# The last mixer's projection issued in pieces between its attention steps, and two modulation sums issued between stages

## The chip, the cores and the metric

The kernel runs on one core of a Trainium2 chip. The metric is the device time of one execution in microseconds (us), as the median of several executions; lower is better. In the profile PE is TensorE (matmul; PEld its weight loads), DVE VectorE, ACT ScalarE, POOL GpSimd and SP SyncE, which only issues DMAs here.

## The reference

256 tokens of width 1024 pass through two blocks in f32. The first has two layers, each of a feed-forward, a mixer (HGRN2 in the first layer, forgetting attention, "Fox", in the second) and another feed-forward. The second block is one layer whose norms are modulated by a vector `c`: feed-forward, token mixer, feed-forward. Each of its three sublayers gets shift, scale and gate from `silu(c) @ w_ada + b_ada`:

```python
u = rms_norm(h, norm_pre[i]) * (1 + scale) + shift
h = h + resid_w * gate * rms_norm(fn(u), norm_post[i])
```

The token mixer projects `u` to 5120 columns (`qa, ka, va` of 512, `qd, kd, vd` of 512, `ga, gd` of 1024) and runs two attentions:

```python
ya = stick_breaking_attention(qa, ka, va)      # 8 heads of 64
yd = rms_norm(softmax(q1 k1) v - lam * softmax(q2 k2) v) * (1 - lambda_init)   # 4 heads, value width 128
merged = sigmoid(ga) * (ya @ w_branch_sb) + sigmoid(gd) * (yd @ w_branch_da)
return merged @ w_out
```

The stick-breaking weights need for every score a softplus and a suffix sum over the keys, then an exponential. The differential attention is the difference of two softmaxes with a bias by distance.

## The kernel before, in words

Everything is written out by hand: each engine has one queue of instructions in program order, and semaphores join them. The list of stages (`plan`, L106) is feed-forward, `hg_in`, `hg_out`, feed-forward, feed-forward, `fox_in`, `fox_out`, feed-forward, feed-forward, `tm_in`, `branch`, `tm_out`, feed-forward. The change concerns the end of two feed-forwards (those before `fox_in` and `tm_in`), the head of `fox_in`, and `tm_in` with `branch`.

**A product in three matmuls.** A weight tile of f32 is split: ScalarE rounds `raw` to `w_hi` (L1231, 128x2048), VectorE computes `w_lo = raw - w_hi` (L1714), or GpSimd does so for a few tiles (L479). Activations are split in the same way (`actT_hi`, `actT_lo`). `three` (L542) then issues `hi*w_hi`, `hi*w_lo` and `lo*w_hi` (L544 to L546), 512 columns each. There are four slots of 128x2048 for `raw`, `w_hi` and `w_lo`. SP refills a slot of `raw` once its `w_lo` is made (`free`); ScalarE rounds into `w_hi` again once TensorE is done with the slot (`split_used`).

**A chunk** is 512 output columns of a projection: 2 token tiles x 8 k x 3 = 48 matmuls, with two slots. Even chunks use slots 0 and 1, odd ones 2 and 3. `proj` (L731) runs chunks one after another; the results are copied from PSUM to `tm_p` in SBUF by ScalarE (token tile 0, L1375) and VectorE (tile 1, L1881).

**The Fox mixer** (L900) already has its projection in pieces: `unit(c, t)` is one token tile of one chunk, 24 matmuls, and attention steps stand between units.

**The last mixer.** `tm_in` runs eight chunks in a row in `proj`. Only then does `token_mixer` (L1046) transpose queries and keys (L1057) and start the stick-breaking attention: scores (L1071), softplus on ScalarE (L1575 to L1577) and VectorE (L2189, L2190), suffix sum on TensorE (L1085), mask on VectorE (L2196), exponentials on ScalarE (L1583, L1584), weighing by the values (L1096). Chunks 8 and 9 (the gate `gd`) are issued in eight half-size parts between these steps, in PSUM banks 6 and 7:

```python
gates(3)
for j in range(4):
    if j == 2:
        gates(1)
    sb_suffix(j)
    gates(1)
    sb_weigh(j)
    if j + 2 < 4:
        sb_scores(j + 2)
```

Then come the four heads of the differential attention: scores (L1130, L1132), biased maxima (L2215 to L2220), exponentials (L1612), the difference of the two (L2226 to L2233), transposition (L1144), copy (L1621) and weighing (L1152). There is no other product among them. One branch product follows, the norm of `yd` and its transposition, then the other three branch products (24 matmuls each) and the gating of all results on VectorE (L2268 to L2271), behind one wait for each half. `tm_out` begins with the transposition of the gated result. GpSimd makes `w_lo` for the gate chunk's slots 2 and 3, the four branch slots and the first two slots of `tm_out`.

**The modulation** (`w_ada`) is summed by GpSimd in three pieces, in the background. `ada_reduce(piece)` (L774) turns a piece's sums into columns with 24 matmuls of one column (L782), and VectorE's `modulation` (L1760) adds bias and norm weight. Pieces 0, 1 and 2 are reduced behind the second chunk of the stages with `norm` 3 (a feed-forward), 4 (`fox_in`) and 6 (a feed-forward). `gate_wide_row` (L786) spreads a gate over all partitions. Between two stages TensorE transposes the first normed token tile (`turn_next`, L552), and waits until ScalarE (L1251 or L1245) and VectorE (L1739, L1742 or L1729) have made the two halves of `actT`.

## Time and profile before

| | us |
|---|---|
| median of 3 executions | 1776.73 |
| lowest, highest | 1772.1, 1778.73 |
| the profiled execution | 1771.41 |
| its span, first to last instruction | 1769.7 |
| TensorE busy (matmul) | 1677.7 |
| VectorE busy | 1012.8 |
| ScalarE busy | 825.3 |
| GpSimd busy | 607.4 |
| mean granted clock of TensorE | 0.974 |

All rows come from the profiled execution. Its time is 1.7 us over its span, and 5.3 us under the median. The clock is given as a share of 2.4 GHz; it has two levels, 1.0 and 0.5 (1.2 GHz). A matmul's own duration (0.39 us) overlaps with the next one's, so costs are read from the distance of starts. The last mixer's first product starts at 1333.7, its second chunk ends at 1365, its eighth at 1430.1; `tm_out` starts at 1538.7 and its last product ends at 1568.1.

### The profile page before, as it was taken

How to read it: one execution, taken by the hardware profiler on the slowest of the kernel's cores; microseconds unless marked ns; L12 is line 12 of the kernel's file. 1: busy time of each engine (PE TensorE's matmuls, PEld its weight loads, DVE VectorE, ACT ScalarE, POOL GpSimd, SP SyncE). 2: the span in 40 equal slices, each digit the busy share in tenths (PEclk: the TensorE clock that was granted, in tenths of full speed). 3: DMA queues.
4: the chain of work that ended last, by engine and by line, in shares of the span. 5: the costliest groups of instructions: out<-in, count | busy, mean ns of one | idle time of the engine just before them, and what ended most of it. 6: DMA issues, size and time to landing. Idle time of an engine off the chain costs nothing.

```text
span 1769.7 us, 21737 instructions
## 1 busy us (share of the span) xinstructions
PE 1677.7 (95%) x7909; PEld 1387.4 (78%) x7909; DVE 1012.8 (57%) x993; ACT 825.3 (47%) x970; POOL 607.4 (34%) x376
## 2 busy tenths in 40 slices
PE   6999999999999999989999999999998986889998
PEld 5888788878887888877887888788876864778886
DVE  4554568676556555666657565645456425465454
ACT  5555552353445344445455443534444355454443
POOL 0000000088888888860018898500000021500000
PEclk9999999999999999989999999999998997899999
DMA  6656453267776677852437778365554521326552
GB/s 215 214 189 197 159 190 107 84 210 253 246 258 218 219 236 243 272 170 96 144 100 236 240 242 273 128 199 189 182 197 134 196 99 46 120 95 213 190 182 79
DMA packets 208279, 321.44 MB, mean 182 GB/s; under 512 B 10920, under 2 KB 146402, under 8 KB 208226
## 3 DMA queue, kind: packets, MB, share of 16 engines
q1 hardware_dynamic: 195968, 281.05, 48.4%
q0 software_dynamic: 10512, 38.54, 7.0%
q10 hardware_dynamic: 1746, 1.11, 0.2%
q8 instruction: 36, 0.59, 0.1%
q14 instruction: 17, 0.14, 0.0%
HBM read 319.62 MB, written 1.05 MB: 181 GB/s over the span
## 4 chain that ended last, share of the span: by engine, by line
PE 85%; DVE 8%; ACT 4%; issue 2%; DMA 0%; ACTq 0%; SPq 0%; DVEq 0%
PE ps L544 25%; PE ps L546 24%; PE ps L545 24%; DVE w_lo L1714 3%; PE ps L648 2%; PE ps L844 1%; ACT w_hi L1231 1%; PE ps L590 1%; PE ps L782 1%; DVE x L1780 1%; PE ps L597 1%; ACT arena L1262 1%; PE ps L976 1%; DVE actT_lo L1729 1%; DVE arena L1748 1%
## 5 line engine op out<-in xcount | busy, mean ns | idle before, releaser
L1714 DVE TENSOR_TENSOR w_lo<-raw,w_hi 128x2048 fp32r<-128x2048 f32 x258 | 653.0, 2540 | 328.6 <-ACT w_hi L1231 328.0
L544 PE MATMUL ps<-w_hi,actT_hi 128*128 128x512 f32 x1504 | 603.0, 401 | 22.0 <-DVE actT_lo L1742 7.8
L1231 ACT CAST w_hi<-raw 128x2048 fp32r<-128x2048 f32 x266 | 505.6, 1911 | 193.4 <-PE ps L546 190.8
L546 PE MATMUL ps<-w_hi,actT_lo 128*128 128x512 f32 x1504 | 592.1, 394 | 0.0
L545 PE MATMUL ps<-w_lo,actT_hi 128*128 128x512 f32 x1504 | 591.2, 393 | 0.0
L544 PEld LDWEIGHTS ps<-w_hi,actT_hi 128*128 128x128 f32 x1504 | 286.5, 191 | 82.6 <-DVE actT_lo L1729 9.0
L546 PEld LDWEIGHTS ps<-w_hi,actT_lo 128*128 128x128 f32 x1504 | 285.6, 190 | 61.9
L545 PEld LDWEIGHTS ps<-w_lo,actT_hi 128*128 128x128 f32 x1504 | 286.8, 191 | 57.0
L544 PE MATMUL ps<-w_hi,hT_hi 128*128 128x512 f32 x480 | 187.5, 391 | 2.6 <-DVE hT_lo L1839 2.6
L546 PE MATMUL ps<-w_hi,hT_lo 128*128 128x512 f32 x480 | 186.8, 389 | 0.0
L545 PE MATMUL ps<-w_lo,hT_hi 128*128 128x512 f32 x480 | 186.8, 389 | 0.0
L497 POOL DMA_DIRECT2D arena<-w_ada_dram x72 | 66.7, 926 | 325.8 <-PE ps L552 279.6
L508 POOL TENSOR_TENSOR arena<-arena 128x512 f32<-128x512 f32 x72 | 161.8, 2247 | 5.6
L505 POOL TENSOR_TENSOR arena<-arena,c_silu 128x1024 f32<-128x1024 f32 x72 | 152.8, 2123 | 11.8 <-DMA arena<-w_ada_dram 9.4
L479 POOL TENSOR_TENSOR w_lo<-raw,w_hi 128x2048 fp32r<-128x2048 f32 x8 | 36.7, 4601 | 341.7 <-ACT w_hi L1231 341.6
L1328 ACT CAST hT_hi<-ps 128x512 fp32r<-128x512 f32 x60 | 35.2, 587 | 233.9 <-PE ps L648 233.9
L510 POOL TENSOR_TENSOR arena<-arena 128x256 f32<-128x256 f32 x72 | 119.5, 1660 | 5.6
L544 PEld LDWEIGHTS ps<-w_hi,hT_hi 128*128 128x128 f32 x480 | 90.1, 188 | 21.6 <-DVE hT_lo L1839 3.0
L546 PEld LDWEIGHTS ps<-w_hi,hT_lo 128*128 128x128 f32 x480 | 90.1, 188 | 18.9
L545 PEld LDWEIGHTS ps<-w_lo,hT_hi 128*128 128x128 f32 x480 | 90.1, 188 | 18.5
L1839 DVE TENSOR_TENSOR hT_lo<-ps,hT_hi 128x512 fp32r<-128x512 f32 x60 | 41.4, 691 | 94.8 <-ACT hT_hi L1328 94.8
L1334 ACT ACTIVATE gate<-ps 128x256 f32<-128x256 f32 x66 | 25.3, 384 | 148.9 <-PE ps L546 130.2
(254 smaller groups left out, 1397.4 us busy)
## 6 DMA issues: line engine op xcount, KB each, us to landing
raw<-ffn_w_in_dram SPq DMA_DIRECT2D x176, 512.0 KB, 4.8
raw<-ffn_w_out_dram SPq DMA_DIRECT2D x88, 512.0 KB, 4.4
arena<-w_ada_dram POOLq DMA_DIRECT2D x72, 512.0 KB, 5.4
raw<-ffn_w_gate_dram SPq DMA_DIRECT2D x44, 512.0 KB, 4.0
raw<-ffn_w_up_dram SPq DMA_DIRECT2D x44, 512.0 KB, 4.9
raw<-ffn_w_down_dram SPq DMA_DIRECT2D x44, 512.0 KB, 4.3
raw<-w_in_dram SPq DMA_DIRECT2D x40, 512.0 KB, 4.5
raw<-hg_w_in_dram SPq DMA_DIRECT2D x32, 512.0 KB, 4.7
```

Of the source, the lines that this page charges most:

```text
L479: nc.gpsimd.tensor_tensor(w_lo[:, s, :], raw[:, s, :], w_hi[:, s, :].bitcast(F32), ALU.subtract)\
L497: nc.gpsimd.dma_start(ada_raw[:, s, :, :], w_ada[:, :, bass.ds(piece * ADA_W + u * ADA_U, ADA_U)])\
L505: nc.gpsimd.tensor_tensor(r, r, c_silu[:, :].unsqueeze(2).to_broadcast([P, KD, ADA_U]), ALU.mult)\
L508: nc.gpsimd.tensor_tensor(r[:, 0:4, :], r[:, 0:4, :], r[:, 4:8, :], ALU.add).then_inc(ada_by4, 1)
L510: nc.gpsimd.tensor_tensor(r[:, 0:2, :], r[:, 0:2, :], r[:, 2:4, :], ALU.add).then_inc(ada_by2, 1)
L544: nc.tensor.matmul(to, hi, whi, start=start, stop=False, skip_group_check=True)
L545: nc.tensor.matmul(to, hi, wlo, start=False, stop=False, skip_group_check=True)
L546: return nc.tensor.matmul(to, lo, whi, start=False, stop=stop, skip_group_check=True)
L648: last = nc.tensor.transpose(ps[:, HT_BANK, f * T + t * P:f * T + (t + 1) * P], hidden[:, t, f * P:(f + 1) * P], ident)
L1231: nc.scalar.copy(w_hi[:, s, :], raw[:, s, :]).then_inc(hi_ready[s], 1)
L1714: nc.vector.tensor_tensor(w_lo[:, s, :], raw[:, s, :], w_hi[:, s, :].bitcast(F32), ALU.subtract)\
L1839: nc.vector.tensor_tensor(hT_lo[:, :, :], ps[:, HT_BANK, :].rearrange("p (f t) -> p f t", f=2), hT_hi[:, :, :].bitcast(F32), ALU.subtract) ...
```

## The change

`tm_in`, `branch` and the attention become one hand-written order on each engine.

- TensorE issues chunks 2 to 9 as 16 units of 24 matmuls in banks 6 and 7, with attention steps between them, and the branch as eight units of 12 matmuls. The first transposition for `tm_out` stands inside the last of these.
- All `w_lo` of the stage are made by VectorE; GpSimd makes none.
- The results of chunks 8 and 9 are copied like all others and the sigmoids are taken in SBUF, for each half of the gates apart. Gating on VectorE goes by branch unit.
- The stick-breaking result is first copied to SBUF (`ya_raw`), and rounded into `actT_hi` only after the last unit of its token tile, since `actT_hi` is read by the projection till then.
- The buffers of scores and weights move in `arena`, and the branch's weights are loaded in another order of slots (both halves of `w_branch_sb` first).
- `ada_reduce(0)` and `ada_reduce(2)` go from behind the second chunk of two feed-forwards to the end of the feed-forwards before `fox_in` and `tm_in`, after `turn_next`. VectorE's `modulation(0)`, `(1)` and `(2)` go to the mixers' queues.

```diff
@@ SP: the branch's slots
-                        n = slice(COLS * (s // 2), COLS * (s // 2) + COLS)
+                        n = slice(COLS * (s % 2), COLS * (s % 2) + COLS)
...
-                            nc.sync.dma_start(to[:, ks, :], branch_w[s % 2][:, ks, n]).then_inc(raw_loaded[s], 16)
+                            nc.sync.dma_start(to[:, ks, :], branch_w[s // 2][:, ks, n]).then_inc(raw_loaded[s], 16)
@@ GpSimd
-            split_gate_weights(by_name["tm_in"])
-            for s in (0, 2, 1, 3):
-                split_lo(s, by_name["branch"].filled[s])
-            for s in (0, 1):
-                split_lo(s, by_name["tm_out"].filled[s])
@@ TensorE: the sums
             def after_second_chunk(st):
                 if st.norm >= 6:
                     pe.wait_ge(gate_row_ready, st.norm - 6 + 1)
-                if st.norm in (3, 4, 6):
-                    ada_reduce({3: 0, 4: 1, 6: 2}[st.norm])
+                if st.name == "fox_in":
+                    ada_reduce(1)
...
                 turn_next(st, 0)
+                nxt = following[id(st)]
+                if nxt is not None and nxt.kind == "in" and nxt.norm > 1:
+                    ada_reduce(0 if nxt.name == "fox_in" else 2)
@@ TensorE: token_mixer
+                def unit(c, t):
...
+                    i, b = c // 2, c % 2
+                    if c > 2:
+                        pe.wait_ge((kept0, kept1)[t], st.kept + c)
+                    for s in (2 * b, 2 * b + 1):
+                        pe.wait_ge(lo_ready[s], st.filled[s] + i + 1)
+                        for kk in range(4):
+                            k, w = 4 * (s % 2) + kk, slice(kk * COLS, (kk + 1) * COLS)
+                            last = three(ps[:, 6 + t, :], actT_hi[:, k, tok], actT_lo[:, k, tok],
+                                         w_hi[:, s, w], w_lo[:, s, w], k == 0, k == KD - 1)
...
+                first_chunk(st, [acc(0, t) for t in range(TILES)], proj0_done)
+                after_first_chunk(st)
+                pe.wait_ge(lam_one, 1)
+                nc.tensor.matmul(ps[:, 5, 0:1], C["ones"][0:1, :], lam_one_col, start=True, stop=True).then_inc(lam_wide, 1)
+                chunk(st, 0, 1)
+                after_second_chunk(st)
```

The new order on TensorE, one call of the code after another (`wait_kept` and the waits inside the calls left out):

```text
unit(2,0) turn(0,4) turn(512,2) unit(2,1) sb_scores(0) sb_scores(1) unit(3,0) sb_suffix(0) unit(3,1) sb_suffix(1)
sb_weigh(0) unit(4,0) sb_scores(2) sb_weigh(1) unit(4,1) sb_scores(3) unit(5,0) sb_suffix(2) unit(5,1) sb_suffix(3)
sb_weigh(2) unit(6,0) sb_weigh(3) turn(1536,0) turn(2048,2) unit(6,1) da_scores(0) da_scores(1) unit(7,0) da_turn(0)
unit(7,1) da_weigh(0) da_turn(1) da_scores(2) unit(8,0) da_weigh(1) da_scores(3) unit(8,1) da_turn(2) unit(9,0)
da_weigh(2) da_turn(3) unit(9,1) da_weigh(3) branch_unit(0,0,0) (0,1,0) (0,0,1) (0,1,1) turn_yd()
branch_unit(1,0,0) (1,1,0) (1,0,1) (1,1,1) with turn_tile(tm_out, 0) inside
```

On ScalarE (`weights(c)` rounds the two slots of chunk c, `keep(c)` copies its tile 0):

```text
weights(1) keep(0) wide weights(2) keep(1) queries(1) weights(3) keep(2) softplus(0) softplus(1) weights(4) keep(3)
sb_weights(0) weights(5) sb_weights(1) keep(4) softplus(2) weights(6) softplus(3) keep(5) sb_weights(2) weights(7)
sb_weights(3) keep(6) keep_ya() queries(3) weights(8) da_weights(0) da_weights(1) keep(7) turned_probs(0) weights(9)
turned_probs(1) da_weights(2) keep(8) da_weights(3) gates(0) split_hi branch 0, 1 turned_probs(2) keep(9) round_ya(0)
turned_probs(3) load_sqrt round_ya(1) squares split_hi branch 2 std split_hi branch 3 gates(1) split_hi out 0 yd_hi
split_hi out 1 turn(out, 0) turn(out, 1) split_hi out 2, 3 turn(out, 2) turn(out, 3)
```

On VectorE (`weights(c)` makes the two `w_lo` of chunk c, `keep(c)` copies its tile 1, which needs the end of `unit(c,1)`; `gated(n, half, t)` gates a branch unit):

```text
modulation(2) weights(1) keep(0) lambda weights(2) keep(1) keys(2) weights(3) keep(2) softplus(0) softplus(1)
weights(4) mask(0) keep(3) mask(1) weights(5) softplus(2) keep(4) softplus(3) weights(6) mask(2) keep(5) mask(3)
weights(7) keys(4) keep(6) weights(8) biased_max(0) biased_max(1) difference(0) keep(7) difference(1) weights(9)
biased_max(2) keep(8) biased_max(3) difference(2) split_lo branch 0 rest_ya(0) difference(3) split_lo branch 1
keep(9) rest_ya(1) mean gated(0,0,0) normed yd gated(0,1,0) split_lo branch 2 gated(0,0,1) split_lo branch 3
gated(0,1,1) yd_lo split_lo out 0 gated(1,0,0) gated(1,1,0) split_lo out 1 turn(out, 0) turn(out, 1) gated(1,0,1)
gated(1,1,1) split_lo out 2, 3 turn(out, 2) turn(out, 3)
```

In the Fox mixer VectorE's queue now begins with `modulation(0)`, and `modulation(1)` stands where the one call was.

## Rows read from the trace of the kernel before

**Rows 1.** the page, part 4: the chain that ended last, by engine

```profile
PE 85%; DVE 8%; ACT 4%; issue 2%; DMA 0%; ACTq 0%; SPq 0%; DVEq 0%
```

**Rows 2.** windows: us; PE, PEld, DVE, ACT, POOL busy (instructions); clock; DMA share; GB/s

```profile
771.00:925.00 154.00, 150.74 (x785) 126.91 (x786) 93.22 (x98) 77.24 (x125) 20.24 (x12) 0.94 0.38 125
1365.00:1430.10 65.10, 65.10 (x289) 53.75 (x287) 30.55 (x18) 24.05 (x17) 0.00 (x0) 1.00 0.59 203
1430.10:1538.70 108.60, 80.14 (x423) 63.84 (x422) 46.10 (x78) 64.61 (x94) 36.73 (x8) 0.88 0.23 78
1487.00:1510.00 23.00, 14.14 (x56) 10.53 (x57) 11.06 (x28) 11.83 (x28) 9.03 (x2) 0.50 0.13 47
1538.70:1568.10 29.40, 26.99 (x113) 21.70 (x114) 15.95 (x18) 14.76 (x22) 0.00 (x0) 0.90 0.12 36
```

**Rows 3.** waits of PE in 1333 to 1540: total us, times, longest

```profile
PE ps L1144 <- DVE arena L2233: 6.7, 2, 4.2
```

**Rows 4.** ACT in the last mixer: a group, and its timeline (start, us)

```profile
L1231 ACT CAST w_hi<-raw 128x2048 fp32r<-128x2048 f32 x9 | 16.9, 1898 | 2.9 <-PE ps L546 2.9
...
1437.53 0.81 ACT L1575 ACTIVATE arena<-ps 128x768 f32<-128x768 f32 x1 [2.27 <-PE ps L1073]
...
1442.56 0.79 ACT L1575 ACTIVATE arena<-ps 128x768 f32<-128x768 f32 x1
...
1518.50 3.73 ACT L1642 ACTIVATE arena<-arena 128x2048 f32<-128x2048 f32 x2
```

**Rows 5.** timeline of DVE in the last mixer

```profile
1365.68 4.49 DVE L1714 TENSOR_TENSOR w_lo<-raw,w_hi 128x2048 fp32r<-128x2048 f32 x2
...
1430.48 0.69 DVE L1881 COPY arena<-ps 128x512 f32 x1 [5.79 <-PE ps L546]
...
1481.05 0.95 DVE L2215 TENSOR_TENSOR arena<-ps,arena 128x768 f32<-128x768 f32 x1
...
1483.15 0.95 DVE L2215 TENSOR_TENSOR arena<-ps,arena 128x768 f32<-128x768 f32 x1
...
1486.32 0.75 DVE L2233 SCALAR_TENSOR_TENSOR arena<-arena,small 128x128 f32<-128x128 f32 x2
```

**Rows 6.** the chain in the last mixer, a suffix sum (start, us)

```profile
1455.28 1.97 PE ps L1085 x12
```

**Rows 7.** timeline of PE, differential scores of two heads

```profile
1479.43 0.50 PE L1130 MATMUL ps<-arena 64*128 64x128 f32 x4
...
1480.19 0.49 PE L1130 MATMUL ps<-arena 64*128 64x128 f32 x4
```

**Rows 8.** window of PE's clock in the Fox mixer

```profile
899.00:906.00 7.00, 7.00 (x27) 6.13 (x27) 2.66 (x5) 0.00 (x0) 0.00 (x0) 0.52 0.65 208
```

**Rows 9.** groups of the last mixer with GpSimd at work

```profile
L479 POOL TENSOR_TENSOR w_lo<-raw,w_hi 128x2048 fp32r<-128x2048 f32 x8 | 36.7, 4601 | 341.7 <-ACT w_hi L1231 341.6
...
L2271 DVE TENSOR_TENSOR arena<-arena 128x512 f32<-128x512 f32 x4 | 6.2, 1543 | 0.1
```

**Rows 10.** the page, part 6: weight loads, us to landing

```profile
raw<-w_in_dram SPq DMA_DIRECT2D x40, 512.0 KB, 4.5
```

**Rows 11.** the chain at the three modulation sums

```profile
580.03 5.25 PE ps L782 x48
...
787.63 7.72 PE ps L782 x48
...
1147.80 6.22 PE ps L782 x48
```

**Rows 12.** windows behind a sum and at the gaps between stages

```profile
585.00:589.00 4.00, 4.00 (x15) 3.38 (x15) 3.60 (x4) 2.38 (x2) 3.63 (x3) 0.57 0.37 107
757.00:762.00 5.00, 0.58 (x5) 0.34 (x3) 4.71 (x7) 2.35 (x7) 4.06 (x4) 0.73 0.26 61
1327.00:1334.00 7.00, 1.11 (x9) 0.87 (x8) 6.86 (x12) 3.81 (x10) 0.00 (x0) 0.67 0.47 150
1334.00:1340.00 6.00, 6.00 (x16) 4.66 (x16) 2.56 (x6) 0.53 (x2) 0.00 (x0) 0.53 0.01 3
```

More of the change, by code:

```diff
@@ L1157, in token_mixer @@
+                unit(6, 0)
+                sb_weigh(3)
+                wait_kept(5)
+                turn(1536, 0)
+                turn(2048, 2)
+                unit(6, 1)
                 da_scores(0)
                 da_scores(1)
[L1159 to L1166 removed]
@@ L1187, in branch @@
-            def branch(st):
-                branch_part(st, 0, 1)
-                pe.wait_ge(yd_ready, 2)
-                for half in range(HALF):
-                    branch_part(st, 1, half)
+                unit(7, 0)
+                da_turn(0)
+                unit(7, 1)
+                da_weigh(0)
+                da_turn(1)
+                da_scores(2)
+                unit(8, 0)
+                da_weigh(1)
+                da_scores(3)
+                unit(8, 1)
+                da_turn(2)
@@ new lines, in token_mixer @@
+                unit(9, 0)
+                da_weigh(2)
+                da_turn(3)
+                unit(9, 1)
+                da_weigh(3)
+                for t in range(TILES):
+                    for half in range(HALF):
+                        branch_unit(0, half, t)
+                turn_yd()
+                branch_unit(1, 0, 0)
+                branch_unit(1, 1, 0)
+                branch_unit(1, 0, 1)
+                branch_unit(1, 1, 1, lambda: turn_tile(by_name["tm_out"], tm_p[:, :, 3072:4096], 0))
@@ new lines, in gates @@
+                def gates(n):
+                    for t in range(TILES):
+                        act.wait_ge((kept0, kept1)[t], st.kept + 8 + 2 * n)
+                        g = tm_p[:, t, 3072 + n * D:3072 + (n + 1) * D]
+                        nc.scalar.activation(g, g, ACT.Sigmoid).then_inc(tm_gates, 1)
+                weights(1)
+                keep(0)
+                wide(st)
+                weights(2)
+                keep(1)
+                queries(1, 4, tm_qaT)
+                weights(3)
@@ new lines, in token_mixer @@
+                keep(2)
+                softplus(0)
+                softplus(1)
+                weights(4)
+                keep(3)
+                sb_weights(0)
+                weights(5)
+                sb_weights(1)
+                keep(4)
+                softplus(2)
+                weights(6)
+                softplus(3)
+                keep(5)
+                sb_weights(2)
+                weights(7)
+                sb_weights(3)
+                keep(6)
+                keep_ya()
@@ L1644, in vectors @@
+                turn(nxt, 3)
             def vectors():
@@ new lines, in token_mixer @@
+                modulation(2)
+                weights(1)
+                keep(0)
+                dve.wait_ge(lam_wide, 1)
+                nc.vector.tensor_scalar(neg_lam_col, ps[:, 5, 0:1], -1.0, None, ALU.mult).then_inc(lam_ready, 1)
+                weights(2)
+                keep(1)
+                keys(2, 2, tm_kaT)
+                weights(3)
+                keep(2)
+                softplus(0)
+                softplus(1)
+                weights(4)
+                mask(0)
+                keep(3)
@@ L2236, in token_mixer @@
+                mask(1)
+                weights(5)
+                softplus(2)
+                keep(4)
+                softplus(3)
+                weights(6)
+                mask(2)
+                keep(5)
+                mask(3)
+                weights(7)
+                keys(4, 2, tm_kdT)
+                keep(6)
+                weights(8)
                 dve.wait_ge(bias_loaded, 16)
-                dve.wait_ge(sb_y, 4)
                 dve.wait_ge(lam_ready, 1)
```

507 lines of the change are left out of this document (245 added, 262 removed).

## The prediction, made before the changed kernel was run

> **What bounds the kernel now.** I read the chain that ended last first, to see which engine sets the end: it is TensorE for 85% of the span [rows 1]. So a microsecond counts only if TensorE waits less, runs less at the lower of its two clocks, or has less to do. Then I read windows of the last mixer. In the last six chunks of its projection TensorE is never idle: 288 matmuls of 512 columns in 65.1 us [rows 2] are 0.226 us each, 5.4 us for a "unit" of 24 (one token tile of one chunk of 512 columns). Behind them come 108.6 us in which TensorE is busy for 80.1, so idle for 28.5, at a mean clock of 0.88 [rows 2]. Most of the low clock (0.5, which is 1.2 GHz) lies in 1487 to 1510: 14.1 us of work at 0.50 [rows 2], of which half, 7 us, is lost, and some 1 us more at the edges. Together **36.5 us are lost** in a stage with about 72 us of work. The waits say why: the attention's exponentials, maxima and masks on ScalarE and VectorE are a serial chain, and TensorE has only two gate chunks and the first branch product to put between its links. The longest are at the transposes of the probabilities, L1144: 6.7 us behind VectorE's difference [rows 3], and one of 6 us beside it.
>
> **Part 1, the projection in pieces.** Nothing is added to TensorE: the same 480 projection and 96 branch matmuls, the same small steps. What changes is that the gaps can be filled with 16 units instead of 8 half-size pieces. The gain is 36.5 us less what the new order still loses. I walk the three written queues with durations of this trace.
>
> Durations: ScalarE rounds a weight slot in 1.9 us, and a softplus step (magnitude, exponential, logarithm, two table loads) takes 5.0 (1437.53 to 1442.56) [rows 4]. VectorE subtracts a slot in 2.25 us and copies a tile of 512 columns in 0.7; a biased maximum takes 2.1 us (1481.05 to 1483.15), a maximum and a difference together 3.9 (to 1487.07), so 1.8 for the difference [rows 5]. The suffix sum takes TensorE 2.0 us [rows 6], the differential scores of a head 0.76 [rows 7].
>
> Stick-breaking part. TensorE puts unit 3,0, suffix 0, unit 3,1 and suffix 1 (14.9 us) between the scores of the second pair of heads and the first weighing. The other side needs two softplus steps (10, begun 0.8 earlier), chunk 4's weights (3.8 on ScalarE, the last 2.25 on VectorE behind it), then a mask (0.7) and exponentials (0.9): 17. TensorE waits 2.1 there and 0.6 before suffix 0. From there to unit 6,0 I find every step early.
>
> Differential part. Here the order is tight, because VectorE now also has all the low halves.
> - After unit 6,1, VectorE has a copy (0.7), two slots (4.5), two maxima (4.2) and a difference (1.8): 11.2. TensorE has two scores (1.5) and unit 7,0 (5.4). It waits 4.3 at the first transposition.
> - After unit 7,1: copy and difference (2.5) against a weighing (about 0.7): 1.8.
> - After unit 8,1: copy, maximum, difference (4.6) against nothing, since the transposition of head 2 comes next: 4.6.
> - After unit 9,0: ScalarE's queue holds the last exponentials (about 2), the first sigmoids (1.3 load, and 1.9, half of the 3.7 of [rows 4]), two slots (3.8) and a copy ahead of what TensorE wants: 1.6. Then copy, rounding of the first attention's result, its low half and a difference, over two engines: 3.1.
> - Before the second branch product, ScalarE's second sigmoids and one slot stand ahead of the rounding of the turned result: 1.5.
>
> These are **19.6 us of waiting**, against 36.5 lost before: 16.9 gained. TensorE's clock then falls where it has too little to do. A fall in the Fox mixer lasted all of 899 to 906 [rows 8], 7 us, 3.5 lost. For my waits I take 5 us, between 0 (no fall) and 10 (three falls). Net 11.9.
>
> GpSimd's eight low halves (4.6 us each [rows 9]) go to VectorE as eight more of 2.25, 18 us; VectorE was busy for 46 of 108.6 and 31 of 65.1 us [rows 2], so it is full only in the places above. While GpSimd ran, a 128x512 addition on VectorE averaged 1.5 us [rows 9], where a copy of the same size takes 0.7; the walk takes every duration from stretches without GpSimd. The Trainium skill, SBUF — State Buffer, "Who interferes with whom", has the two engines lock one port pair; rows 9 agree, and it speaks for the change.
>
> Weight transfers move with the low halves that free their slots; by the walk a slot is free 10 us or more before its next rounding, against 4.5 us for landing [rows 10], so I cost them at nothing. SP's queue keeps its order of slots. If one came late, its unit would wait for all of the lateness.
>
> The first output product starts hot, with its source already turned inside the last branch unit. Of its 29.4 us, at a clock of 0.90 [rows 2], I take off 4: 0.90 is 6 us at the low level, 3 lost, and some 1 of waiting for weights and residual. The lambda matmul and the maxima's bias load only change place.
>
> **Part 2, two modulation sums moved.** The 24 one-column matmuls took 5.25 us at 580 and 6.22 at 1147.8 on the chain [rows 11]. The clock fell behind the first (585 to 589 at 0.57 [rows 12]: 3.4 us low, 1.7 lost); I take the same for the second. Removed: 14.9. Their new place is the gap between feed-forward and mixer, where TensorE waits for the turned activations (it is busy for 0.58 of 757 to 762 and 1.11 of 1327 to 1334 [rows 12]). The means of 0.73 and 0.67 there put the fall of the clock at 759.3 and 1329.4. At 787.63 the same 24 took 7.7 us [rows 11], with the fall inside them at about 790.5; that makes 0.22 each before it (as at 580) and 0.43 behind. Started at 757.2 and 1327.6, 10 and 8 run before the fall and the rest behind it: they end about 3.5 and 2.6 us after the moment (761.8, 1333.7) at which the product starts now. Bounds: nothing at all, and 5.9 and 4.4 (all at the low rate, 10.3). I take 6.1, so part 2 gives 8.8. VectorE's three small operations per sum go to the head of its mixer queue; they take well under 1 us, and chunk 1's low halves are ready over 1 us early, so nothing, and 1 us if not.
> The Trainium skill, TensorE: Matmul & The Clock Gate, "What's actually happening", says that the throttle is the default state and activity releases it. Taken so, the sums would hold the clock up through the gap. Rows 11 and 12 don't agree: it fell during or right behind such sums. It is a rival below.
>
> **Sum.** 11.9 + 4 + 8.8 = 24.7 off the profiled execution's 1771.4 gives 1746.7. That execution lies 5.3 under the median of the three runs, 1776.7, so the median should be **1752**.
>
> **Rivals.**
> - *TensorE stays fed.* The Fox mixer has the same form, and in 154 us TensorE is idle for only 3.3 there at a clock of 0.94 [rows 2] (18 us low, 9 lost): 12 lost. If this mixer did as well, the 24.6 that I leave it become 12: gain 37, 1739. Against it: my waits are sums of rows on one queue.
> - *The sums keep the clock up.* They end 0.6 us late at most, and the 4 to 5 us at the low level behind each gap (1334 to 1340 at 0.53 [rows 12]) go too, half of it gained: 5.5 and 4.6, some 10 more, 1742. Against it are the falls at 585 and 790.
> - *Falls of clock everywhere.* Each of eight waits brings a 7 us fall: 28 lost instead of 5, the change is worth 2, 1775.
> - *Slower.* VectorE becomes the bound of every chunk: low halves stand behind softmax steps that themselves wait for TensorE's next step, so slots, of which each has one buffer, are freed late in turn. Place: chunks 2 to 9. Were each to wait for one unit and a rounding (5.4 + 1.9), 58 us would be lost, against 49 that there are to win (36.5, 4, 8.8): 1786. It decides from 6.2 us per chunk. VectorE's busy shares above speak against it.
>
> **Chances.** Forecast (gain 13 to 33) 0.60, fed 0.20, clock held 0.08, falls everywhere 0.07, slower 0.05. The measurement can tell about 0.5%, 9 us. The range goes from the fed case with the sums hidden (37 and 6: 1733) to the upper costs of clock (5 more), gaps (4) and a slip of 8 in the walk: gain 8, 1769. Faster 0.88, same 0.07, slower 0.05.
>
> **What would show it.** In the profile after: waits of about 4, 2, 5 and 3 us at the probabilities' transposes, released by VectorE's difference, and one near 2 at the first weighing; GpSimd idle after its sums; from the end of chunk 1 (1365.0) to the first output product 162 us instead of 173.7; the moved sums in the gaps, with the product 3 us later behind them. Wrong it would be if TensorE hardly waits, if a transfer is what releases units, or if the clock stays low after the first wait.

## The result, and the profile of the changed kernel

The changed kernel takes **1752.3 us** (median of 4 executions, 1750.6 to 1754.6) against 1775.4 for the kernel before in the same session (4 executions): a ratio of 0.9875, 95% interval 0.9855 to 0.9895, so 23 us less (19 to 26). A second session (e11 below) gave 0.9858 (0.9832 to 0.9885). The forecast was 1752. But it was not right term by term, and the runs below show why. The profiled execution takes 1751.1 us with a span of 1749.4. Against the profiled execution before (1771.4) that is 20.3 us less: 6.7 up to the end of chunk 1, 8.7 in the mixer, 4.0 in the output product and 0.9 behind it.

The page's chain of work that ended last, by engine, answers to [rows 1]:

```profile
PE 64%; POOL 20%; DVE 6%; issue 5%; ACT 3%; POOLq 1%; DMA 0%; ACTq 0%; SPq 0%; DVEq 0%
```

It says 20% for GpSimd where it had none. TensorE is as busy as ever (1678.1 us, 96%). What is new is one link in the Fox mixer, at which TensorE waits for GpSimd. Behind it the chain follows GpSimd's own work back for hundreds of microseconds. The share is large, but its price is only the wait, 0.42 us in this execution (below).

Windows of the changed kernel; the columns are those of [rows 2]. The first runs from the end of chunk 1 to the first output product, which were 173.7 us in the kernel before. The second is the output product, 29.4 before. The last two are the stretches of the two gaps:

```profile
1358.30:1523.30 165.00, 147.70 (x709) 119.04 (x708) 88.32 (x101) 91.25 (x115) 0.00 (x0) 0.93 0.37 126
...
1523.30:1548.70 25.40, 23.91 (x114) 19.68 (x113) 17.88 (x22) 15.06 (x22) 0.00 (x0) 1.00 0.23 74
...
750.00:770.00 20.00, 19.45 (x97) 16.92 (x95) 8.09 (x19) 5.94 (x20) 17.02 (x15) 0.74 0.45 140
1318.00:1345.00 27.00, 24.82 (x112) 21.23 (x113) 19.05 (x34) 11.86 (x25) 0.60 (x1) 0.75 0.20 69
```

In the mixer TensorE is idle for 17.3 us (165.0 less 147.7), where it was for 28.5. Yet it is busy for longer than the 145.2 us of before (65.10 and 80.14 in [rows 2]), with the same work: the clock costs more than it did. The stretches at the low level between 1358.3 and 1523.3 of the changed kernel are these, with the one such stretch of the mixer before behind them (windows of two kernels):

```profile
1390.60:1394.00 3.40, 3.40 (x13) 2.50 (x10) 2.19 (x1) 3.40 (x3) 0.00 (x0) 0.50 0.88 330
1445.20:1452.00 6.80, 5.11 (x14) 4.15 (x15) 1.53 (x6) 2.77 (x10) 0.00 (x0) 0.50 0.12 47
1458.80:1462.30 3.50, 3.50 (x11) 2.36 (x8) 3.50 (x3) 0.06 (x1) 0.00 (x0) 0.51 0.32 90
1475.90:1482.70 6.80, 4.47 (x12) 3.68 (x13) 2.13 (x8) 6.17 (x12) 0.00 (x0) 0.50 0.00 0
1489.60:1493.00 3.40, 3.03 (x9) 2.55 (x10) 2.52 (x2) 1.97 (x3) 0.00 (x0) 0.50 0.12 44
```

```profile
1486.40:1510.30 23.90, 14.45 (x57) 10.75 (x58) 11.96 (x29) 12.43 (x30) 9.03 (x2) 0.50 0.13 45
```

TensorE was busy for 19.5 us at half speed, so 9.7 us were lost; before it was 14.4 us, so 7.2 were lost. The same work at the full clock takes 138.0 us by either kernel (147.7 less 9.7, 145.2 less 7.2). The output product starts hot, at a clock of 1.00, and takes 25.4 us.

Waits of PE from 1315 to 1560 in the changed kernel (us in total, times, longest), which answer to [rows 3]:

```profile
PE ps L1096 <- DVE arena L2245: 13.2, 4, 4.6
...
PE ps L1072 <- ACT arena L1574: 1.9, 1, 1.9
PE ps L532 <- DVE actT_lo L2337: 1.7, 1, 1.7
PE ps L1059 <- DVE arena L2211: 0.5, 1, 0.5
```

L1096 is the transposition of the probabilities, L2245 VectorE's difference. One by one, from the timeline of PE (start, us, the wait and its releaser in brackets):

```profile
1446.89 0.90 PE L1096 MATMUL ps<-consts_sb,arena 128*128 128x128 f32 x3 [3.80 <-DVE arena L2245]
...
1457.79 0.55 PE L1096 MATMUL ps<-consts_sb,arena 128*128 128x128 f32 x3 [1.84 <-DVE arena L2245]
...
1478.23 0.90 PE L1096 MATMUL ps<-consts_sb,arena 128*128 128x128 f32 x3 [4.61 <-DVE arena L2245]
...
1489.97 0.90 PE L1096 MATMUL ps<-consts_sb,arena 128*128 128x128 f32 x3 [2.97 <-DVE arena L2245]
```

The walk had 4.3, 1.8, 4.6 and 3.1. The reader should also see the 0.90 us that three of the four transpositions take, against 0.55 for the other: they run at the low clock.

VectorE in the mixer, now without GpSimd beside it (groups from 1358 to 1523, columns as in [rows 9]). The addition of the gated halves, 128x512 with both sources in SBUF, is back at 0.69 us from 1.54. The multiplications ahead of it, with one source in PSUM (L2263), take the 0.68 that they took beside GpSimd before (L2268 and L2269 there):

```profile
L1741 DVE TENSOR_TENSOR w_lo<-raw,w_hi 128x2048 fp32r<-128x2048 f32 x20 | 45.1, 2287 | 8.0 <-ACT w_hi L1240 7.9
...
L2263 DVE TENSOR_TENSOR arena<-arena,ps 128x512 f32<-128x512 f32 x6 | 4.1, 686 | 2.8 <-PE ps L534 2.8
...
L2267 DVE TENSOR_TENSOR arena<-arena 128x512 f32<-128x512 f32 x2 | 1.4, 692 | 0.1
```

The two sums that stayed visible, piece 1 in the Fox mixer and piece 2 in its new gap, from the chain; they answer to [rows 11]:

```profile
788.98 6.55 PE ps L740 x48
...
1319.37 7.25 PE ps L740 x48
```

### The profile page after: what moved, and what is told of

It reads as the page before. It is cut to its first block, busy times and chain, and to the rows that moved or that the text cites. A ratio compares the mean times of both kernels' runs of the same rounds, so it can differ in the third digit from the quotient of the medians.

```text
span 1749.4 us, 21688 instructions
## 1 busy us (share of the span) xinstructions
PE 1678.1 (96%) x7909; PEld 1387.5 (79%) x7909; DVE 1022.2 (58%) x1003; ACT 826.2 (47%) x973; POOL 570.5 (33%) x368
## 4 chain that ended last, share of the span: by engine, by line
PE 64%; POOL 20%; DVE 6%; issue 5%; ACT 3%; POOLq 1%; DMA 0%; ACTq 0%; SPq 0%; DVEq 0%
PE ps L532 18%; PE ps L534 18%; PE ps L533 18%; POOL arena L501 6%; POOL arena L498 6%; POOL arena L503 4%; POOL arena L505 3%; DVE w_lo L1741 2%; PE ps L802 1%; PE ps L638 1%; POOL arena L490 1%; ACT w_hi L1240 1%; PE ps L578 1%; PE ps L740 1%; PE ps L934 1%
## 5 line engine op out<-in xcount | busy, mean ns | idle before, releaser
L1741 DVE TENSOR_TENSOR w_lo<-raw,w_hi 128x2048 fp32r<-128x2048 f32 x266 | 668.8, 2524 | 333.2 <-ACT w_hi L1240 333.1
L532 PE MATMUL ps<-w_hi,actT_hi 128*128 128x512 f32 x1504 | 605.1, 402 | 10.1 <-DVE actT_lo L1756 3.2
L503 POOL TENSOR_TENSOR arena<-arena 128x256 f32<-128x256 f32 x72 | 115.9, 1609 | 5.6
L1869 DVE TENSOR_TENSOR hidden<-gate,ps 128x256 f32<-128x256 f32 x132 | 54.3, 416 | 54.4 <-ACT gate L1343 48.0
```

Of the source, the lines that this page charges most:

```text
L503: nc.gpsimd.tensor_tensor(r[:, 0:2, :], r[:, 0:2, :], r[:, 2:4, :], ALU.add).then_inc(ada_by2, 1)
L532: nc.tensor.matmul(to, hi, whi, start=start, stop=False, skip_group_check=True)
L1741: nc.vector.tensor_tensor(w_lo[:, s, :], raw[:, s, :], w_hi[:, s, :].bitcast(F32), ALU.subtract)\
L1869: nc.vector.tensor_tensor(hidden[:, t, :], gate[:, t, :], ps[:, UP_BANK + t, FC:COLS], ALU.mult)\
```

## The experiments

Each ratio is to the kernel before, run in the same session; 0.001 is 1.8 us. "Changed" is the changed kernel.

| run | what | median us | ratio, 95% |
|---|---|---|---|
| changed | | 1752.3 | 0.9875 (0.9855 to 0.9895) |
| e11 | changed again | 1753.7 | 0.9858 (0.9832 to 0.9885) |
| e1 | part 2 alone (sums) | 1766.2 | 0.9949 (0.9928 to 0.9971) |
| e2 | part 1 alone (mixer) | 1759.7 | 0.9912 (0.9898 to 0.9926) |
| e3 | transpositions later | 1735.6 | 0.9779 (0.9763 to 0.9794) |
| e4 | e3, difference first | 1732.1 | 0.9738 (0.9720 to 0.9757) |
| e5 | low halves on GpSimd | 1762.9 | 0.9922 (0.9904 to 0.9939) |
| e6 | wide matmuls among the sums | 1756.0 | 0.9897 (0.9879 to 0.9915) |
| e7 | e2, gaps filled wide | 1754.3 | 0.9871 (0.9848 to 0.9894) |
| e8 | modulation behind low halves | 1754.3 | 0.9870 (0.9840 to 0.9901) |
| e9 | e8, piece 1 shortened | 1747.7 | 0.9831 (0.9815 to 0.9847) |
| e10 | e4's orders on e7 | 1733.6 | 0.9757 (0.9739 to 0.9775) |
| e12 | waits filled wide | 1742.7 | 0.9823 (0.9802 to 0.9844) |

e11 is the changed kernel without an edit, in the session of e9, e10 and e12:

> The changed kernel once more, unchanged, as the common measure of the experiments: ratio 0.9875 to the kernel before, within 0.002. If its ratio comes out outside of that, the differences of 2 to 4 us between the experiments (e6, e7, e8 against the changed kernel) are not to be read.

Measured: within 0.002, so the table can be read down to some 3 us, and no finer.

For the mixer there is a second measure, the time from its first transposes to those ahead of the output product. It was 157.46, 157.40 and 157.49 us in the traces of changed, e2 and e11. But it isn't always the same: in e8, whose orders in the mixer and whose four waits at the transpositions (3.80, 1.83, 4.61, 2.98) are those of changed, it was 152.16, because the clock fell two times instead of five:

```profile
1371.39:1523.55 152.16, 134.83 (x671) 109.02 (x670) 86.74 (x98) 89.63 (x112) 0.00 (x0) 0.97 0.39 132
```

So waiting can be read from a trace to a tenth of a microsecond, but what the clock costs differs between executions by up to some 5 us.

**Do the parts add up? e1 and e2.** e1 has only the moved sums, with VectorE's operations on them (not shown here):

```diff
-                if st.norm in (3, 4, 6):
-                    ada_reduce({3: 0, 4: 1, 6: 2}[st.norm])
+                if st.name == "fox_in":
+                    ada_reduce(1)
...
+                if nxt is not None and nxt.kind == "in" and nxt.norm > 1:
+                    ada_reduce(0 if nxt.name == "fox_in" else 2)
```

> The kernel before with part 2 alone: the modulation sums of pieces 0 and 2 stand behind the feed-forward stages, and VectorE's three operations for each stand at the head of its queue in the next mixer; the mixer is as before. If the two parts add up, and the mixer's new order does not need the moved sums, this gives what the trace of the changed kernel shows at the four places: 6.9 us removed and some 4.5 given back in the Fox mixer, 8.4 removed and 1.2 given back at the last mixer, so about 9.6 us off the kernel before (ratio about 0.995); the prediction had 8.8. Rival: the moved sums also bring the low clock forward into the first chunk, and that part of the saving of the changed kernel which lies in the last mixer's first chunk came from the new order; then 5 us or less (ratio 0.997 or more).

e2 is the changed kernel with just that undone.

> The changed kernel with part 2 undone: the sums of pieces 0 and 2 stand again behind the second chunk of the feed-forward stages. If the parts add up, this is slower than the changed kernel by the 9.6 us of part 2, so some 13 us off the kernel before (ratio about 0.9925): 8.6 in the mixer and 4.1 in the output product. The prediction had 15.9 for the two. Rival: the two parts overlap (both take from the same low clock in the first chunk of the last mixer), and this alone gives over 17 us.

Measured: 9.1 us (5 to 13) and 15.6 us (13 to 18). The sum, 24.7, lies between the two measurements of both together (22 and 25), so no overlap of the parts can be seen, within intervals of 3 and 4 us. The part sizes of the prediction were 8.8 and 15.9.

**The waits at the transpositions: e3 and e4.** e3 changes only TensorE's order:

```diff
                 unit(7, 0)
-                da_turn(0)
                 unit(7, 1)
+                da_turn(0)
+                unit(8, 0)
                 da_weigh(0)
                 da_turn(1)
                 da_scores(2)
-                unit(8, 0)
+                unit(8, 1)
                 da_weigh(1)
                 da_scores(3)
-                unit(8, 1)
-                da_turn(2)
                 unit(9, 0)
+                da_turn(2)
+                unit(9, 1)
                 da_weigh(2)
                 da_turn(3)
-                unit(9, 1)
                 da_weigh(3)
```

> The changed kernel, on TensorE alone in another order of the same steps: of each head's transposition of the probabilities and its weighing, every one stands about one projection unit later (unit 7,1 ahead of the transposition of head 0, the scores of head 2 behind unit 8,0, the transposition of head 2 behind unit 9,0 with unit 9,1 behind it). If the waits at the transpositions (13.2 us in four) are VectorE's queue being half a unit to a unit behind, they fall to about 4, and the clock falls once or twice less: 9 to 13 us below the changed kernel (ratio to the kernel before about 0.981). Rival 1: exponentials, difference, transposition and copy are a chain of fixed length that TensorE waits for whole at its end; then the wait moves to the last weighing or the first branch product, and the time stays within 2 us of the changed kernel. Rival 2: most is lost by the clock after any wait, however short; then the waits fall but 24 us at the low clock stay, and the gain is some 5.

Measured: 17 us below changed by the ratio (0.9779 against 0.9875), 14 against e11. That is more than the expectation asked, and both rivals are out. The waits of PE at L1096 went from 13.2 us in four to one:

```profile
PE ps L1096 <- DVE arena L2245: 2.5, 1, 2.5
```

The same stretch with the same 672 matmuls, from the first transposes to those ahead of the output product, in changed and in e3 (windows of two kernels):

```profile
1363.71:1521.17 157.46, 140.16 (x672) 112.70 (x670) 86.75 (x98) 89.76 (x112) 0.00 (x0) 0.92 0.37 127
```

```profile
1368.55:1508.37 139.82, 132.58 (x672) 107.55 (x670) 86.92 (x98) 89.21 (x112) 0.00 (x0) 0.99 0.42 143
```

It is 17.6 us shorter: 10.1 of them are waiting (17.3 less 7.2), and 7.6 are the same matmuls in less busy time at a clock of 0.99 instead of 0.92. Of the 7.6, 1.7 belong to the fall at 1390 in changed, behind the first weighing, where e3 altered nothing: the wait of 1.9 us there was followed by a fall in six of the twelve traces with this mixer (changed, e2, e4, e6, e9, e11) and by none in the others. That leaves some 6 for the moved steps, so a wait here cost about 1.6 times its length. By e8 it can be less: behind the same 13.2 us of waits TensorE lost 4.0 us by the clock there, where it lost 8.0 in changed.

e4 puts VectorE's last difference first as well:

```diff
+                difference(3)
                 split_lo(0, mix.filled[0])
                 rest_ya(0)
-                difference(3)
```

> The kernel with the later transpositions (e3), and on VectorE the difference of head 3 ahead of the low half of the first branch slot and of the first attention's low halves, instead of behind them. In e3 TensorE still waited 2.5 us for that difference and 0.6 for the copy behind it. If that wait is the queue order, it goes (2.5 to 3 us below e3, whose median was 1735.6). Rival: the low halves that now come later are what the first branch unit needs, and it waits there for as long: no change, or 1 us slower.

Measured: 3.5 us below e3 by the medians, 7 by the ratios of two sessions; in the trace the stretch is 137.06 us instead of 139.82, so 2.8. The queue order was the cause of the wait of 2.5, and the first branch unit did not wait. The 0.6 us behind it stayed.

**What the clock costs by itself: e12.** TensorE waits as before, but does useless wide work meanwhile:

```diff
                 def da_turn(h):
+                    pe.wait_ge(da_max, h + 1)
+                    for _ in range((14, 6, 16, 10)[h]):
+                        nc.tensor.matmul(ps[:, 2 * (h % 2), :], hT_hi[:, 0, 0:P],
+                                         hT_hi[:, :, :].rearrange("p f t -> p (f t)"), start=True, stop=True)
                     pe.wait_ge(da_p, 2 * (h + 1))
```

> The changed kernel with 14, 6, 16 and 10 useless 512-column matmuls (3.2, 1.4, 3.6 and 2.3 us at the full clock) in the four waits at the transpositions of the probabilities (3.8, 1.8, 4.6 and 3.0 us), so that TensorE is busy while the same differences are awaited. This separates what a wait costs by itself from what the clock costs behind it: if the four falls between 1446 and 1493 (20 us at the low clock, some of it inside the waits) come from the waits, they go, and the kernel is 4 to 8 us faster than the changed one with as long a wait for VectorE. Rival: the narrow steps around the waits are enough for the falls; then the fillers run at the low clock too, last longer than the waits, and the kernel is up to 3 us slower.

Measured, in the same session as e11: 6 us below it by the ratios, 11 by the medians. The stretch takes 149.79 us, 7.7 less, at a clock of 1.00:

```profile
1357.43:1507.22 149.79, 142.23 (x717) 114.29 (x716) 86.74 (x98) 89.56 (x112) 0.00 (x0) 1.00 0.39 134
```

So none of the 9.7 us that the clock took in changed are lost here: 8.0 of them lay behind the four waits, and 1.7 behind the first weighing, where nothing was filled and this trace has no fall. Some 2 us of the gain went again, since the fillers with the waits that are left take longer than the waits took: TensorE still waits 2.0 us at the transpositions, and 1.5 at a weighing where it didn't in changed. That the 7.7 here and the 7.6 of e3 are so close is chance.

**Queue length or shared port: e5.** GpSimd makes the low halves of chunks 8 and 9:

```diff
+            for s in range(SLOTS):
+                n = by_name["tm_in"].filled[s] + 4
+                pool.wait_ge(hi_ready[s], n + 1)
+                nc.gpsimd.tensor_tensor(w_lo[:, s, :], raw[:, s, :], w_hi[:, s, :].bitcast(F32), ALU.subtract)\
+                    .then_inc(lo_ready[s], 1)
...
-                weights(8)
...
-                weights(9)
```

> The changed kernel with the low halves of the last two projection chunks (8 slots' worth in two chunks: 4 subtractions of 2.25 us on VectorE) made by GpSimd again, 4.6 us each and out of VectorE's queue. If VectorE's queue length makes the waits at the probabilities' transpositions (4.6, 4 and so on: 13.2 in four), the first and the one behind chunk 9's weights each lose up to 4.5 us, so about 5 to 8 us of waiting go and the time falls by as much. Rival: VectorE runs slower while GpSimd runs (a 128x512 operation took 1.5 us instead of some 0.7 in the kernel before), and the copies, maxima and differences of this stretch give back most of it: 0 to 3 us faster, or slower.

Measured: 8 to 11 us slower than changed, as the rival had it ("or slower"). The waits grew to 19.4 us. The first fell from 3.8 to 3.0, the second grew from 1.8 to 8.9, and the other two stayed:

```profile
PE ps L1101 <- DVE arena L2250: 19.4, 4, 8.9
```

The timelines of GpSimd and VectorE in e5, and of VectorE for the same head in changed, tell why (start, us, operation):

```profile
1456.68 8.98 POOL L529 TENSOR_TENSOR w_lo<-raw,w_hi 128x2048 fp32r<-128x2048 f32 x2 [8.59 <-ACT w_hi L1245]
```

```profile
1457.97 0.17 DVE L2243 RECIPROCAL small<-small 128x4 f32<-128x4 f32 x1
1458.17 3.06 DVE L2244 TENSOR_SCALAR small<-small 128x2 f32<-128x2 f32 x1
1461.26 4.74 DVE L2247 TENSOR_SCALAR arena<-arena,small 128x128 f32<-128x128 f32 x2
1466.04 0.75 DVE L2250 SCALAR_TENSOR_TENSOR arena<-arena,small 128x128 f32<-128x128 f32 x2
```

```profile
1455.93 0.17 DVE L2238 RECIPROCAL small<-small 128x4 f32<-128x4 f32 x1
1456.13 0.23 DVE L2239 TENSOR_SCALAR small<-small 128x2 f32<-128x2 f32 x1
1456.40 0.55 DVE L2242 TENSOR_SCALAR arena<-arena,small 128x128 f32<-128x128 f32 x2
1456.99 0.75 DVE L2245 SCALAR_TENSOR_TENSOR arena<-arena,small 128x128 f32<-128x128 f32 x2
```

An operation on 128x2 elements takes 3.06 us instead of 0.23: it ends at 1461.2, where the first of GpSimd's two subtractions ends, and the next stands until the second has ended near 1465.7. VectorE isn't slowed in proportion, it is held until GpSimd's instruction is over. The Trainium skill, SBUF — State Buffer, "Who interferes with whom", says of VectorE's two-port modes that whoever issues first has the shared pair for the whole instruction and the other "fully blocks". This trace agrees as to the blocking; in which mode the operations ran it doesn't show.

**The gaps: e6 and e7.** e6 puts a useless 512-column matmul behind every third sum:

```diff
+                    if fill and u % 3 == 1:
+                        nc.tensor.matmul(ps[:, UP_BANK, :], hT_hi[:, 0, 0:P],
+                                         hT_hi[:, :, :].rearrange("p f t -> p (f t)"), start=True, stop=True)
```

> The changed kernel, with a 512-column matmul of no use (feed-forward values on both sides, into a bank that nothing reads) behind every third of the 24 one-column matmuls of the two moved sums: 8 more per sum, 1.8 us at the full clock. If one-column matmuls and waiting are what lets TensorE's clock fall in these gaps, and wide matmuls hold it, the sum with its filler ends after 7.1 us (now 7.55 and 7.25) and the first chunk behind it runs at the full clock instead of losing some 3 us: 5 to 8 us below the changed kernel in all. Rival: the clock falls as before, by the wait or by the share of narrow work; then each sum takes 1.8 to 3.5 us more, all of it behind the moment at which the activations are there: 3 to 7 us slower than the changed kernel.

Measured: 0.9897, so 4 us slower than changed, or 7 than e11. The intervals overlap, so "slower" isn't shown; but the gain of 5 to 8 us isn't there. The traced execution is the fastest of e6's four (1747.8). Even in it the clock falls inside the mixed stretch of the second gap, which begins at 1316 (windows of e6):

```profile
1316.00:1320.00 4.00, 4.00 (x29) 3.77 (x29) 3.93 (x7) 1.25 (x4) 0.00 (x0) 0.87 0.45 123
1320.00:1329.00 9.00, 9.00 (x34) 8.04 (x34) 4.56 (x12) 2.58 (x7) 0.60 (x1) 0.50 0.26 76
```

e7 has the sums in their old places and 26 such matmuls, one behind the other, in each gap:

```diff
                 turn_next(st, 0)
+                if st.norm in (3, 6):
+                    for _ in range(26):
+                        nc.tensor.matmul(ps[:, UP_BANK, :], hT_hi[:, 0, 0:P],
+                                         hT_hi[:, :, :].rearrange("p f t -> p (f t)"), start=True, stop=True)
```

> The kernel with only the mixer's part of the change (e2), with 26 useless 512-column matmuls, 5.9 us at the full clock, in the two gaps between feed-forward stage and mixer in place of waiting; the sums stand in their old places. If it is the idle time there, or the narrow work of the sums, that lets the clock fall, it now stays up through the gap and the first chunk behind it: 3 to 7 us less in each gap, 1750 to 1753 against 1759.7 for e2. Rival: the fall is already caused by the wait of 1.7 us and the eight transposes at the end of the feed-forward stage, ahead of the filler; then the filler itself runs partly at the low clock, ends after the moment at which the activations are there, and the time is equal to that of e2 or up to 4 us more.

Measured: 1754.3 against 1759.7 for e2 in another session (5 us less; 0.9871 against 0.9912, 7 us less). The clock stays up through both gaps; these windows of e7 answer to the 0.74 and 0.75 shown above. The 0.94 is a fall from 1340 on, behind a later wait of 1.9 us; until then the second one has 1.00:

```profile
750.00:770.00 20.00, 20.00 (x98) 16.58 (x97) 9.85 (x20) 8.27 (x23) 16.89 (x15) 1.00 0.59 184
1318.00:1345.00 27.00, 23.37 (x100) 18.05 (x99) 20.59 (x35) 14.62 (x31) 0.00 (x0) 0.94 0.21 71
```

The wait of 1.7 us and the eight transposes ahead of the filler are the same in e7 as in changed, so they didn't bring the fall by themselves; it came where narrow sums (changed) or idle time (e2) stood behind them. The Trainium skill, TensorE: Matmul & The Clock Gate, "What's actually happening", says that activity releases the throttle. With wide matmuls that agrees; with one-column matmuls, and with three of them to one wide one, TensorE was busy for some nine tenths of the time or more in the rows here, and the clock fell.

**What became of the gain in the Fox mixer: e8 and e9.** e8 changes VectorE's order, for piece 0 and piece 2 alike:

```diff
-                modulation(0)
                 weights(1)
+                modulation(0)
                 keep(0)
```

> The changed kernel with VectorE's three operations on the sums of pieces 0 and 2 behind the low halves of the mixer's second chunk instead of ahead of them. In the changed kernel's Fox mixer TensorE waited 1.6 to 1.9 us for a low half in chunk 1, which the prediction had at nothing. If these operations at the head of the queue (they wait for the end of the sum, and hold the low halves back) are the cause, the wait goes, and the kernel is up to 2 us faster. Rival: the low halves are late because VectorE runs slower beside GpSimd there; then the wait stays as it was.

Measured: the same time as changed. In changed the first product on those low halves waited 1.58 us, and VectorE's three small operations took 3.0 (timelines of PE and VectorE):

```profile
777.37 0.50 PE L532 MATMUL ps<-w_hi,actT_hi 128*128 128x512 f32 x1 [1.58 <-DVE w_lo L1741]
```

```profile
770.94 0.17 DVE L1790 TENSOR_TENSOR modc<-ps,cols 128x24 f32<-128x24 f32 x1
771.14 2.66 DVE L1793 SCALAR_TENSOR_TENSOR mod_scale<-modc,cols 128x8 f32<-128x8 f32 x1
773.83 0.17 DVE L1795 SCALAR_TENSOR_TENSOR mod_gate<-modc,cols 128x8 f32<-128x8 f32 x1
```

The second began while GpSimd issued a transfer (770.90 to 771.83), and stood until the multiplication behind it, which ran from 771.85 to 773.76, had ended. So both stories have part of it: the operations are at the head of the queue, and they are slow beside GpSimd. It depends on the moment. In six of the eight traces with this order the second operation took 2.25 to 2.66 us and TensorE waited 1.1 to 1.6. In e11, which is the same kernel, and in e4 it fell between two of GpSimd's instructions, and TensorE didn't wait (VectorE in e11):

```profile
770.12 0.17 DVE L1790 TENSOR_TENSOR modc<-ps,cols 128x24 f32<-128x24 f32 x1
770.32 0.17 DVE L1793 SCALAR_TENSOR_TENSOR mod_scale<-modc,cols 128x8 f32<-128x8 f32 x1
770.52 0.17 DVE L1795 SCALAR_TENSOR_TENSOR mod_gate<-modc,cols 128x8 f32<-128x8 f32 x1
```

With e8's order that wait is gone too, but the time came back, a small part in the last mixer (0.9 us before the matmuls that spread the gate, L748, for `mod_gate`, which now comes later), most of it at the next wait, the sums of piece 1, which wait for GpSimd. The timeline of PE there in changed, e11 and e8:

```profile
788.98 6.55 PE L740 MATMUL ps<-consts_sb,arena 128*128 128x1 f32 x48 [0.42 <-POOL arena L505]
```

```profile
788.16 10.40 PE L740 MATMUL ps<-consts_sb,arena 128*128 128x1 f32 x48 [2.28 <-POOL arena L505]
```

```profile
792.48 10.40 PE L740 MATMUL ps<-consts_sb,arena 128*128 128x1 f32 x48 [6.74 <-POOL arena L505]
```

Near the end of the Fox mixer nothing is left of what the first moved sum gave: transposes which stand there in both kernels begin at 906.72 in the traces of before and of changed alike.

e9 shortens GpSimd's last two partial sums of piece 1. It leaves out seven eighths of the products in these two, so its modulation isn't that of the reference, and its time is only a bound for what is to be had here:

```diff
-                    ada_unit(piece, ADA_N // 2 - 1, s)
+                    ada_unit(piece, ADA_N // 2 - 1, s, piece == 1)
```

> The kernel with VectorE's modulation operations behind the low halves (e8), and the last two of GpSimd's 24 partial sums of piece 1 computed from a small part of their data (an eighth of the products, and the additions over them shortened alike), so that this part of the last mixer's modulation is left out; GpSimd ends piece 1 some 5 us earlier. In the changed kernel and in e8 TensorE waited 0.4 and 6.7 us for GpSimd at the sums of piece 1 (0.4 to 6.7 in the ten traces), and the clock was low for up to 20 us behind that. If GpSimd is what caps the gain of part 2 in the Fox mixer, that wait goes and the time is 5 to 8 us below e8 (1754.3): 1746 to 1749. Rival: TensorE meets another wait within the next steps (the forget gates' chain on ScalarE and VectorE), or the clock falls by the narrow sums alone: within 2 us of e8.

Measured: 1747.7, 7 us below e8 by the ratios, and in the same session 6 below e11 by the medians, 5 by the ratios. The intervals overlap in either comparison, so the size isn't sure. In its trace PE doesn't wait at these sums, though they still take 7.85 us, partly at the low clock; that is its slowest execution (1754.7), and TensorE waits 2.5 us for `mod_gate` in the last mixer. So GpSimd's piece 1 is what the earlier TensorE runs into; that its removal is worth 5 to 7 us is likely, but not shown. Where the wait is 2.3 us or more, the sums behind it take 10.40 us, all at the low clock, instead of 6.55.

Executions of one kernel with moved sums lie up to 19 us apart (e1: 1758.1 to 1777.4; e11: 1744.6 to 1759.6), those of the kernel before within 9 in a session. The moments at GpSimd may be one cause, the falls of the clock in the mixer (e8) another; e7, without moved sums, has 11 us too. Only one execution of each has a trace, so that stays open.

**The best of both: e10.** e7 with the orders of e3 and e4.

> All together but the moved sums: later transpositions and the earlier difference (e4), and the wide useless matmuls in the two gaps with the sums in their old places (e7). e7 was as fast as the changed kernel, so moving the sums and holding the clock are worth the same; if the parts add up this takes what e4 took, 1731 to 1735. Rival: e7 was at its time only by the clock's luck, and this is 1737 or more.

Measured: 1733.6, as added up. Against e4 the ratios differ by 0.002, less than their intervals. e4 and e10 both beat both kernels, by 2.6% and 2.4% to the kernel before. e4 is the simpler one, and computes nothing useless.

## Why the prediction was right, point by point

- **The total.** 24.7 us forecast, 23 measured by the medians; by parts 15.9 and 8.8 against 15.6 and 9.1, with intervals of some 3 and 4 us. That the median comes out at 1752 itself is partly luck. The sum was made for the profiled execution, 1746.7, and that took 1751.1: 20.3 us less, not 24.7 (mixer 8.7 for 11.9, output product 4.0 for 4, before them 6.7 for 8.8). The 5.3 us which were put on for the median were 1.2 in the changed kernel. Where the medians gained the rest no trace shows.
- **The mixer's waits.** 19.6 us forecast, 17.3 idle. The four at the transpositions were 3.80, 1.84, 4.61, 2.97 for 4.3, 1.8, 4.6, 3.1; the first weighing 1.9 for 2.1, suffix 0 0.5 for 0.6, the second branch product 1.7 for 1.5. Only the 1.6 before the weighing of head 2 didn't come. The cause was right too: e3 and e4 took the waits at the transpositions away by order alone.
- **The clock in the mixer: the term that was mis-sized.** "For my waits I take 5 us, between 0 (no fall) and 10": it took 9.7 in the traces of changed and e11, 8.0 of it behind the four waits. Its upper bound was three falls of 7 us; there were five, of 3.4 or 6.8 us. In e8 it took 4.0 with the same waits, so within its bounds the term is also a matter of the execution. The 8 us taken for the kernel before were 7.2. So 35.7 us were lost before (28.5 and 7.2) and 27.0 after (17.3 and 9.7). Idle time gave 11.2 instead of 8.9, and the clock took 2.5 instead of giving 3: 8.7 instead of 11.9.
- **The output product.** 4 forecast, 29.4 to 25.4 measured, at a clock of 1.00 as said.
- **The sums in the gaps.** Ends 3.5 and 2.6 us late forecast. At the last mixer the transposes ahead of the gap came 8.4 us earlier (1318.28 for 1326.71: sum 2 removed, 7.9 forecast) and the first product 7.2 earlier (1326.48 for 1333.69): 1.2 late. In the Fox mixer those transposes came 4.4 earlier and the product 1.6 (760.17 for 761.76): 2.8 late. (The upper bounds of 5.9 and 4.4 come to 5.7 and 4.2 by their own terms; nothing rests on that.) The fall of the clock inside the sums came as said, and "the sums keep the clock up" is out.
- **"They take well under 1 us ... so nothing".** The step that failed, in six of eight traces. Beside GpSimd the three operations took 3.0 us in changed, and TensorE waited 1.58; in e11 and e4 they took 0.5 and it didn't. The prediction kept "1 us if not" for this, and had the contention in [rows 9], but used it only for large operations.
- **What is late next, in the Fox mixer.** The prediction moved a sum from ahead of a GpSimd-bound one without asking when GpSimd would be done. TensorE didn't wait there in the trace of before; in the nine traces with the moved sums and all of GpSimd's work it was 0.4 to 6.7. In the trace of changed the whole gain of the first moved sum is gone by the end of the Fox mixer. What part 2 gave there (7.2 us at the first product of the last mixer) is the other sum, whose gap cost less (1.2 for 2.6) and whose removal was worth more. So that part 2 alone measured 9.1 us (5 to 13) for the 8.8 forecast is in part two errors which offset each other.
- **The rivals.** "TensorE stays fed" (1739) was wrong of this order, but e4 shows that an order exists which does that, and more: 1732. "Falls everywhere" came in part: five falls behind seven waits, but they cost 9.7 us and not 28. "VectorE bounds every chunk" didn't occur; no transfer released a unit.

## What to carry to other kernels

Where an order of queues is written by hand, walk each queue with measured durations, then move the consumer of a serial chain behind one more piece of independent work: one unit later was worth 14 to 17 us here, because a wait of TensorE cost its length and a third to two thirds of it again by the clock. When a stage gets shorter, look for the engine whose work ends at a fixed time whatever TensorE does (here GpSimd's partial sums): it caps the gain. And don't hand work to GpSimd beside a chain of small VectorE operations, even if VectorE's queue is the bound.

## What the runs showed of the hardware that was not expected

- A VectorE operation on 128x2 elements took 3.06 us (e5) and one on 128x8 took 2.66 (changed) beside GpSimd's instructions on SBUF, against 0.23 (changed, GpSimd idle) and 0.17 (e11, between two of GpSimd's) otherwise; a 128x4 reciprocal next to the first took its 0.17 all the same, and 128x512 operations with one source in PSUM took 0.68 with GpSimd beside them and without.
- After four waits of 1.8 to 4.6 us the clock was low for 20 us of 48 (1446 to 1494 of changed has a granted clock of 0.80), and so in six of the seven traces with these waits; in the seventh (e8) it was low for 10. The same time filled with 512-column matmuls had 1.00 throughout (e12).
- The clock fell during 24 one-column matmuls, though TensorE shows no idle time in them, and also with 8 wide ones among them (e6). During 26 wide ones it didn't (e7).
